# Weights kept as a bf16 copy in DRAM and reloaded from it, instead of being cast from fp32 at every load

## The reference

```python
h = rmsnorm(x, norm_mix_g);  u = h @ w_in                  # 1024 -> 1536
y_conv = silu(layernorm(dwconv31(val * sigmoid(gate))))    # u[:, :1024]
y_pool = per-group linear(trailing mean over 2/4/8/16 - v) # u[:, 1024:]
x = x + concat(y_conv, y_pool) @ w_out
h = rmsnorm(x, norm_xattn_g);  mem_n = rmsnorm(mem, norm_mem_g)
k, v = split(mem_n @ w_kv);  x = x + attention(h @ w_q, k, v) @ w_o   # 256 memory tokens
h = rmsnorm(x, norm_ffn_g)
gate, val = split(dwconv3(h @ w_up))                       # 1024 -> 2 * 2816
x = x + (silu(gate) * val) @ w_down
out = rmsnorm(x, norm_final_g)
```

## Time and profile before

| | us |
|---|---|
| median of 2 runs | 2509.98 (2507.18 to 2512.78) |
| the profiled execution, whole | 2509.8 |
| span of its slowest core, core 3 | 2508.3 |
| spans of the eight cores | 2499.9 to 2508.3 |

### The profile page before, as it was taken

How to read it: one execution, slowest core, us unless ns; L and a number is a source line. 1 busy time by engine, 2 the same in 40 slices (tenths; PEclk the granted TensorE clock), 3 DMA queues, 4 the chain that set the end, 5 groups by cost and what they waited for, 6 DMA issues and landing times.

```text
span 2508.3 us, 28697 instructions; the slowest of 8 cores (2499.9 to 2508.3 us)
## 1 busy us (share of the span) xinstructions
PE 1998.1 (80%) x8992; PEld 901.1 (36%) x8992; DVE 1502.8 (60%) x2009; ACT 1147.1 (46%) x2271; POOL 131.2 (5%) x254
## 2 busy tenths in 40 slices
PE   0599787999679787899728978799984997879995
PEld 0343333443234333344314433334432433334432
DVE  0142476888742365888833335678885424768887
ACT  0323425665632434655633243356656234256554
POOL 5300000000000000000000000000000000000000
PEclk9899898999789887999958988789997998989998
DMA  8610216352511034433263103235245101133531
GB/s 183 99 34 1 31 20 101 51 89 38 138 64 34 1 51 64 85 54 56 75 164 68 34 0 51 38 68 97 39 72 168 34 1 24 28 51 51 80 48 67
DMA packets 91044, 153.67 MB, mean 61 GB/s; under 512 B 3088, under 2 KB 52368, under 8 KB 90896
## 3 DMA queue, kind: packets, MB, share of 16 engines
q0 software_dynamic: 80816, 115.48, 28.7%
q1 hardware_dynamic: 10080, 36.36, 4.0%
HBM read 250.53 MB, written 16.78 MB: 107 GB/s over the span
## 4 chain that ended last, share of the span: by engine, by line
PE 50%; DVE 23%; ACT 12%; issue 9%; another core or an unknown queue 2%; DMA 2%; DVEq 0%; POOL 0%; ACTq 0%; SPq 0%; POOLq 0%
PE pmb L412 47%; DVE t L836 5%; DVE t L839 5%; DVE t L717 4%; DVE t L442 3%; ACT t L827 3%; ACT t L826 2%; PE ptb L439 2%; ACT t L435 1%; DVE t L880 1%; DVE t L848 1%; PE pmb L614 1%; PE pmb L616 1%; DVE t L862 1%
## 5 line engine op out<-in xcount | busy, mean ns | idle before, releaser
L412 PE MATMUL pmb<-t,t 128*128 128x512 bf16 (+1 forms) x8064 | 1852.3, 392 | 275.8 <-DVE t L848 80.9
L412 PEld LDWEIGHTS pmb<-t,t 128*128 128x128 bf16 x8064 | 803.6, 101 | 1316.6 <-issue 470.7
L836 DVE SCALAR_TENSOR_TENSOR t<-t,t,t 128x512 f32<-128x512 f32 x352 | 263.3, 748 | 84.3 <-ACT t L827 60.5
L839 DVE SCALAR_TENSOR_TENSOR t<-t,t,t 128x512 f32<-128x512 f32 x352 | 264.3, 751 | 38.5 <-DVE t L836 2.3
L827 ACT ACTIVATE t<-pmb,t 128x512 f32<-128x512 f32 x352 | 276.2, 785 | 0.0
L862 DVE TENSOR_TENSOR t<-pmb,t 128x512 f32<-128x512 f32 x384 | 252.6, 687 | 35.0 <-PE pmb L412 15.3
L439 PE MATMUL ptb<-t,t 128*128 128x128 bf16 x800 | 97.2, 298 | 220.8 <-ACT t L435 178.2
L826 ACT COPY t<-pmb 128x512 f32<-128x512 f32 x352 | 206.6, 587 | 104.0 <-PE pmb L412 74.4
L416 ACT ACTIVATE t<-t 128x1024 bf16<-128x1024 f32 x64 | 67.6, 1056 | 254.7 <-DVE t L732 150.6
L439 PEld LDWEIGHTS ptb<-t,t 128*128 128x128 bf16 x800 | 74.4, 134 | 252.6 <-issue 252.4
L442 DVE TENSOR_TENSOR t<-ptb,t 128x1024 bf16<-128x1024 bf16 x100 | 122.5, 1225 | 58.8 <-PE ptb L439 51.3
(11 more groups left out here) (76 smaller groups left out, 856.6 us busy)
## 6 DMA issues: line engine op xcount, KB each, us to landing
t<-w_up POOLq DMA_DIRECT2D x32, 1024.0 KB, 12.8
t<-x SPq DMA_DIRECT2D x32, 512.0 KB, 6.4
t<-w_down POOLq DMA_DIRECT2D x16, 1024.0 KB, 19.7
out<-t SPq DMA_DIRECT2D x32, 512.0 KB, 3.3
t<-w_in POOLq DMA_DIRECT2D x4, 3072.0 KB, 37.6
t<-w_up POOLq DMA_DIRECT2D x16, 768.0 KB, 10.1
t<-w_kv POOLq DMA_DIRECT2D x2, 4096.0 KB, 44.1
t<-w_out POOLq DMA_DIRECT2D x4, 2048.0 KB, 15.4
```

The costliest lines, as they stand in the source:

```text
L412: S.op("pe", lambda e, l=l, r=r, i=i: e.matmul(bank_ap, lhsT=l, rhs=r, start=(i == 0), stop=(i == n - 1)), reads=list(reads) + list(extra_ ...
L836: S.op("dve", lambda e, U=U, a=a, ch=ch: e.scalar_tensor_tensor(out=a, in0=U[:, 1:513], scalar=vcol(V_FW + ch * 3 + 1), in1=a, op0=ALU.mul ...
L839: S.op("dve", lambda e, U=U, a=a, ch=ch: e.scalar_tensor_tensor(out=a, in0=U[:, 0:512], scalar=vcol(V_FW + ch * 3 + 0), in1=a, op0=ALU.mul ...
```

## The change

Each weight block is loaded from the fp32 original once, on its first use (`w_in`, `w_q`, `w_kv`, `w_out`, `w_o`, and the six FFN passes `p0` to `p5`), on POOL's queue as before. After that it is stored from SBUF, as it lies there (bf16, 128 partitions, each a contiguous row), into a DRAM tensor of its own, `sc_<key>`. Every later load is one plain DMA from that tensor, issued on SP's queue. Also, `x` of group 0 and `w_in` of group 0 are now appended at the top of group 0, with `x` ahead of `mem` on SP's queue.

The stores are appended to SP's list by `flush_stores`, at the start of the next call of `wload`: the store of `w_in` stands on SP directly ahead of `mem` of group 0. A store waits until its load has landed, and the load that next overwrites the same buffer waits until the store has landed.

```diff
-        def load_w(slot, dst, src, R, extra=()):
-            S.dma("pool", slot, dst, src, writes=R, extra=extra)
-
-        load_w(slots["wa"], w_in_v, kp(dw_in), [RWA])
+        scr = {}
+        pend_st = []
+
+        def flush_stores():
+            while pend_st:
+                key_, flat_, R_ = pend_st.pop(0)
+                sc_, Rsc_, ssl_ = scr[key_]
+                S.dma("sp", ssl_, sc_, flat_, reads=R_, writes=[Rsc_])
+
+        def wload(key, slot, flat, parts, R):
+            flush_stores()
+            if key not in scr:
+                scr[key] = (nc.dram_tensor("sc_" + key, [128, flat.shape[1]], BF16).ap(), Res(), S.newslot("st_" + key))
+                for dst_, src_ in parts:
+                    S.dma("pool", slot, dst_, src_, writes=R)
+                pend_st.append((key, flat, R))
+            else:
+                sc_, Rsc_, ssl_ = scr[key]
+                hslot = {id(slots["wa"]): slots["wa_h"], id(slots["wb0"]): slots["wb0_h"], id(slots["wb1"]): slots["wb1_h"]}[id(slot)]
+                S.dma("sp", hslot, flat, sc_, reads=[Rsc_], writes=R)
+
+        def load_w_in():
+            wload("w_in", slots["wa"], WA[:, 0:12288], [(w_in_v, kp(dw_in))], [RWA])
+
+        def load_w_q():
+            wload("w_q", slots["wa"], WA[:, 0:8192], [(w_q_v, kp(dw_q))], [RWA])
+
+        def load_w_kv():
+            wload("w_kv", slots["wb0"], WB[:, 0:16384], [(w_kv_v, kp(dw_kv))], [RWB0, RWB1])
+
+        def load_w_out_o():
+            wload("w_out", slots["wb0"], WB[:, 0:8192], [(w_out_v, kp(dw_out))], [RWB0])
+            wload("w_o", slots["wb1"], WB[:, 12288:20480], [(w_o_v, kp(dw_o))], [RWB1])
...
+            if gi == 0:
+                issue_x(0, range(NT))
+                load_w_in()
             if first:
-                load_w(slots["wb0"], w_kv_v, kp(dw_kv), [RWB0, RWB1])
+                load_w_kv()
...
-                load_w(slots["wb0"], w_out_v, kp(dw_out), [RWB0])
-                load_w(slots["wb1"], w_o_v, kp(dw_o), [RWB1])
-
-            if gi == 0:
-                issue_x(0, range(NT))
+                load_w_out_o()
+
...
-                load_w(sl, g_[:, :, 0:n * 128], kp(dw_up)[:, :, j0 * 128:(j0 + n) * 128], R)
-                load_w(sl, v_[:, :, 0:n * 128], kp(dw_up)[:, :, DFF + j0 * 128:DFF + (j0 + n) * 128], R)
-                load_w(sl, dn_[:, 0:n, :], dw_down.rearrange("(j p) n -> p j n", p=128)[:, j0:j0 + n, :], R)
+                wload("p%d" % p, sl, WB[:, slot * 12288:(slot + 1) * 12288],
+                      [(g_[:, :, 0:n * 128], kp(dw_up)[:, :, j0 * 128:(j0 + n) * 128]),
+                       (v_[:, :, 0:n * 128], kp(dw_up)[:, :, DFF + j0 * 128:DFF + (j0 + n) * 128]),
+                       (dn_[:, 0:n, :], dw_down.rearrange("(j p) n -> p j n", p=128)[:, j0:j0 + n, :])], R)
...
-        S.final_wait("sp", Rout)
+        flush_stores()
+        S.final_wait("sp", Rout + [v_[1] for v_ in scr.values()])
```

More of the change, by code:

```diff
@@ L384, in build_program @@
         slots = {n: S.newslot("d_" + n) for n in
-                 ("c", "x0", "x1", "x2", "x3", "x4", "x5", "x6", "x7", "wa", "wb0", "wb1", "o0", "o1", "o2", "o3", "o4", "o5", "o6", "o7", "mem", "pw")}
+                 ("c", "x0", "x1", "x2", "x3", "x4", "x5", "x6", "x7", "wa", "wb0", "wb1", "wa_h", "wb0_h", "wb1_h", "o0", "o1", "o2", "o3", "o4", "o5", "o6", "o7", "mem", "pw")}
         xslots = [slots["x%d" % i] for i in range(NT)]
@@ L595, in build_program @@
                 S.op("dve", lambda e: e.tensor_copy(utail[:], upT[:, :, 0:16]), reads=[RupT], writes=[Rtail])
-            load_w(slots["wa"], w_q_v, kp(dw_q), [RWA])
+            load_w_q()
             def p1b_conv(b):
```

## The result

| | before | changed |
|---|---|---|
| ratio of the times, 95% interval | 1 | 1.0106 [1.009, 1.0121] |
| median of all runs (10 and 11) | 2514.12 us | 2540.61 us |
| profiled execution | 2509.8 us | 2536.5 us |
| its cores, shortest to longest span | 2499.9 to 2508.3 us | 2513.6 to 2535.0 us |

The kernel became about 26 us slower, 1.1%. The forecast was 2515 us with a range up to 2531: the sign was right, and some 20 us are missing from the sum. (Some executions on all eight cores run several per cent longer at a lower clock, whatever the kernel; apart from the medians of this table, ratios, medians and spans of a die leave them out, no interval is given where too few others were left, and the only profile of such an execution is that of w_in_cast, 2598.53 us.)

What follows compares the result with a forecast made beforehand. Prediction: PE, DVE and ACT set the pace and DMA matters only at the start and the turn into group 2. 2509.8 + 7 (start) - 2 (turn) + 0 elsewhere = 2515 us, range 2502 to 2531.

Steps and rivals of the forecast that it cites:

- What bounds the kernel: Whole kernel: PE, DVE and ACT set the pace; DMA matters only at the start and the turn into group 2.
- R5: Rival, whole kernel: weight traffic slows the engines now, so the change is over 2% faster, 2455 us; chance 0.03.
- R4: Rival, FFN: reloads slower than their window make PE wait, over 2% slower, 2560 us; chance 0.03.
- Term A: Start of group 0, up to the K/V matmuls: 1.9 us plus a delay of 5, +7 us, bounds +2 and +7.2.
- d: Start: delay of w_in's issue because pool_w takes turns with x packets; 0 to 5.3 us, taken as 5.
- x moves out of the way: Start: mem and x no longer share the DMA engines with w_in and w_kv, 3.46 MB, saving 9.1 us.
- the store of `w_in` beside `w_kv`: Start: storing w_in, 3.15 MB, shares the DMA engines with the w_kv load, at 0.38 MB per us: 8.3 us.
- R2: Rival, start and turn: big rows move slowly, at 245 GB/s +10.7 us, 2526 us; at 184, 2536; chance 0.13.
- `mem` in time: Start: mem lands by 64 us and is prepared by 74, ahead of w_kv at 82, so it adds no wait.
- R1: Rival, start: store rows cut into 4 KB packets make mem late, its 8.7 us come on top, 2523 us; chance 0.20.
- Term B: Turn into group 2: x loads start sooner, but mem stands behind w_kv on SP; -2 us, bounds -3 and -1.
- At other places: 0: Rest of the kernel: reloads and group 0's stores stay hidden, FFN units stay 22.75 us apart, 0 us.

Runs made afterwards that it cites:

- w_in_cast: Changed kernel with group 0's mem and x issued in the old order, its stores held until w_kv landed, and w_in cast in every group: ratio 1.0026 [1.0015, 1.0036].
- before_x_first: Kernel before, with only the x loads of group 0 moved ahead of mem on SP's queue: ratio 1.0011 [0.9994, 1.0028], K/V matmuls at 77.9 us.
- old_head: Changed kernel with group 0's mem and x issued as before; stores meant to follow w_kv, but w_in's still ran beside it: ratio 1.0057, K/V at 85.8 us.
- turn_mem_ahead: Changed kernel, with mem issued ahead of w_kv on SP's queue at the turn into group 2: ratio 1.0062 [1.0044, 1.008].
- stores_only: Changed kernel, old mem and x order, stores held until w_kv landed, every load a cast, copies never read: 2535.44 us in one run, against 2530.14 before.

## Why the prediction was wrong, point by point

**What bounds the kernel: right.** The sum had the right two places, start and turn, and no other single place moved by more than a couple of us. A quarter less DMA time gave nothing back, as it said (R5), and no pass was ever waited for (R4): a reload landed in 10.0 us (forecast 8.7), in a window of 37.9.

**Term A, the start: +19.2 instead of +7. The step that failed is the delay d, with its upper bound; the price of the store beside `w_kv` was mis-sized too.** By its own parts, as means over the eight cores:
- *x moves out of the way: -7.6, forecast -9.1* (before_x_first).
- *d, the wait for `pool_w`: 11.0 (12.0 between the two cores shown), forecast 5 with an upper bound of 5.3.* The bound counted 33 turns of 0.16 us, the time that one `x` packet occupies an engine. The measured row is 13.9 us to landing. DMA queues, changed kernel, first the window 12:13, then 15:18:

```profile
q1 hardware_dynamic: 98, 0.36, 97.5%
q0 software_dynamic: 3, 0.00, 0.8%
...
q1 hardware_dynamic: 244, 0.89, 92.6%
q0 software_dynamic: 244, 0.06, 21.9%
```

  Issued at 7.95, `pool_w` moves its first packets just ahead of 13. From then on the turns are equal, as assumed, but each lasts longer than an `x` packet alone: 244 pairs on 16 engines in 3 us are 0.197 us a pair, 33 of them 6.5 us; the last packet starts 8.5 us behind the first. So about 5 us of beginning (1.6 before, where `x` was not in the way) and 6.5 to 8.5 us of turns; the formula had only the turns, and was no bound. Why the beginning takes 5 us no run here shows. The rule of the Trainium skill that I weighed there ("DMA: Bandwidth & Descriptors", "Queues, rings and completion order": a whole packet of several descriptors per turn, d about 1) would have been further off; this trace shows one row to one row.
- *the store of `w_in` beside `w_kv`: 11.0, forecast 3.15 / 0.38 = 8.3* (old_head). The rows are single packets of 24 KB and the turns one to one, the case that I took; the counts of the two queues are equal to one packet in every 2 us from 62 to 70. Window 60:70, DMA queues:

```profile
DMA packets 181, 2.65 MB, mean 265 GB/s; under 512 B 0, under 2 KB 0, under 8 KB 87
...
q1 hardware_dynamic: 93, 2.29, 85.4%
q0 software_dynamic: 87, 0.36, 19.4%
```

  But a packet lasts 0.854 x 16 x 10 / 93 = 1.47 us, not 1.03, and both queues together move 265 GB/s, not 380. That is the rate of R2, "big rows move slowly", though not its reason: without a cast beside it the store of `w_kv`, 4.19 MB in rows of 32 KB, moves at 352 GB/s (window 95:107), so size alone isn't slow; large rows in turns with a cast's are.
- *`mem` on the engines: about 4, forecast 1.05 / 0.38 = 2.8. `mem` in time*: wrong, by about 1 us. The chain of estimates was store issued at 44, through at 55, `mem` there at 64; measured 55.6, 74.8 and 86.2. Each step was short: 6 us by d, 5 by `w_in` itself (24.1 us to land, forecast 18.7), 8 by the store, 2 by `mem`. A margin of 8 us was used up, since `w_kv` was late as well, but not the 8.7 of R1. R1 named the mechanism, and its sign, a wait on `mem` ahead of the K/V matmuls, is there in seven of eight cores; its reason (packets of 4 KB) was wrong.

Together -7.6 + 11.0 + 11.0 + 3.9 + 0.9 = 19.2, as measured: all five parts came out above the forecast's, and d alone makes half of the 12 us that were missing.

**Term B, the turn: between 0 and +1 instead of -2.** The reading was right: the stores and `x` gain, and the gain is spent behind `w_kv`. The rate wasn't. `mem` landed 19.9 us after its issue; the 7.34 MB took 1331.8 - 1307.9 = 24 us, 307 GB/s and not 362 to 405. (The 1.5 us for landing in that sum stand on no row of this case.) turn_mem_ahead shows that the wait for `mem` there is set by the order in the queue.

**Everything else: +5 to 7 instead of 0.** Here the step "At other places: 0" failed. It rested on units at 447.88 and 470.64, whose pace DVE sets, and was then used for the first unit, where PE sets the pace. A sign of being right failed there too: the unit from 448.62 takes 25.43 us and not 22.75. At that place the reloads go with a clock of 1.00 in the first 24 matmuls, a longer wait, more often a clock of 0.50 behind it, and about 1 us lost a group. The statement "a load in flight costs the engines nothing" itself holds there: 5.18 us beside a full load and without one. Why the granted clock differs stays open, and so do the other places, up to about 1 us each, which I can locate but not explain. The stores, forecast 0, are part of the 5 to 7 us on one die at least (stores_only).

**Bytes.** q1 has 158.0 MB, forecast 152: the last two of the six passes load 2.36 MB, and the copy stores and reloads the whole buffer of 3.15 MB. 0.79 x 2 x 4 = 6.3 MB.

**The range** ended at 2531 because both ends of d came from one formula, and because the unknown terms were taken as if independent. They erred the same way: the prices per MB came from rates in which one queue was nearly alone. The sign of the forecast came out right by its start term alone; the turn and the rest had it wrong or at nothing.

## What to carry to other kernels

Before making weights cheaper to load, ask who waits for a load: here it was one wait at the start and one at a turn, and a new order of issue there took 2% off with or without the copy, while the copy with its stores and `x` ahead of the waited-for loads cost 1%. A store is deferred only by something ahead of it on its engine that really waits; look in the trace for the time of its issue. And take the price of a transfer beside another from rows in which two of their kind stand together: here the rates were 15 to 30% lower in company.

## What the runs showed of the hardware that I had not expected

- 128 KB cast through the software queue took 13.9 us to land beside 4.2 MB of plain loads issued ahead of it, against 3 us alone (issued at 6.52, POOL goes on at 9.95). Taking it off POOL's critical list is cheaper than any copy.
- Rows of 24 KB are one packet each, and an engine takes them in turns with the 4 KB packets of the other queue, one to one (93 to 87), which gives the store 86% of the bytes. A store that nobody waits for delays the load that everybody waits for, by 11.0 us for 3.15 MB.
- The same 24 FFN matmuls took 5.18 us at a granted clock of 1.00, with or without a full DMA load beside them, and 6.3 us at 0.81. The faster ones were followed by a longer wait for DVE (3.45 us against 0.8 to 2.9) and in 30 of 42 cores by a clock of 0.50, 2.6 us lost in a unit. Open: what sets 0.81, which 21 of 24 cores with casts had there and no core with reloads alone.
